# Sparse attention by pairs of heads, values as weights, and the output product in the same stage

## What is computed

```python
q, kc, vc, ks, vs, kw, vw, gates = jnp.split(proj, cuts, axis=-1)
k_cmp = partial_rope(compress(kv_heads(kc), ...), cmp_end)      # 31 compressed keys
p_cmp = masked_softmax(q . k_cmp, cmask);  o_cmp = p_cmp . v_cmp
p_slc = masked_softmax(q . k_sel, smask);  o_slc = p_slc . v_sel
p_win = masked_softmax(q . kw_b, wmask);   o_win = p_win . vw_b
o = gb[..., 0:1] * o_cmp + gb[..., 1:2] * o_slc + gb[..., 2:3] * o_win
return o @ w_out
```

## Time and profile before

| | us |
|---|---|
| median of three runs | 2269.97 |
| lowest and highest | 2268.28, 2273.12 |
| the profiled execution: its time | 2268.3 |
| the profiled execution: its span, first to last instruction | 2266.5 |
| TensorE busy (matmuls) | 2038.2 (90% of the span) |
| VectorE busy | 1384.4 (61%) |
| ScalarE busy | 951.4 (42%) |

### The profile page before, as it was taken

The page is one execution under the profiler, slowest core; times in us unless marked ns, Lnnn a source line. Parts: engine busy times, 40 slices in busy tenths (PEclk is TensorE's granted clock), DMA queues, the critical chain, the costliest instruction groups (busy, mean ns, idle before and its releaser), DMA issues. The chain is left out here.

```text
span 2266.5 us, 29883 instructions
## 1 busy us (share of the span) xinstructions
PE 2038.2 (90%) x11912; PEld 1725.2 (76%) x11912; DVE 1384.4 (61%) x1962; ACT 951.4 (42%) x1399; POOL 147.8 (7%) x206
## 2 busy tenths in 40 slices
PE   5999988969999898999979999699968887799996
PEld 5888878869999786776758888578956666588785
DVE  7964545545454454433468999645036665689997
ACT  5653335221111001623457777421125553477774
POOL 3442000000000000000110001000000000010010
PEclk9999998989999999999979999899879999899998
DMA  7433112214232222221429999432420001199993
GB/s 211 111 73 97 57 57 95 75 29 131 75 111 76 75 76 78 96 93 38 140 68 375 390 394 384 157 89 93 117 77 1 1 1 60 58 354 390 389 381 155
DMA packets 161896, 324.48 MB, mean 143 GB/s; under 512 B 30128, under 2 KB 98416, under 8 KB 161632
## 3 DMA queue, kind: packets, MB, share of 16 engines
q1 hardware_dynamic: 133872, 282.92, 35.7%
q0 software_dynamic: 11488, 31.28, 4.3%
q10 hardware_dynamic: 16400, 8.39, 1.5%
HBM read 299.41 MB, written 17.89 MB: 140 GB/s over the span
## 5 line engine op out<-in xcount | busy, mean ns | idle before, releaser
L2289 PE MATMUL ps<-m_ws,m_xbT 128*128 128x512 f32 x1344 | 314.5, 390 | 0.0
L2289 PEld LDWEIGHTS ps<-m_ws,m_xbT 128*128 128x128 f32 x1344 | 251.8, 188 | 52.2
L2520 DVE TENSOR_TENSOR m_ws<-ring,m_ws 128x2048 fp32r<-128x2048 f32 x112 | 256.1, 2290 | 27.0 <-ACT m_ws L2369 16.3
L1630 PE MATMUL ps<-ffT,ff_ws 128*128 128x264 f32 (+1 forms) x1056 | 241.6, 324 | 4.4 <-DVE ff_ws L433 4.4
L2369 ACT CAST m_ws<-ring 128x2048 fp32r<-128x2048 f32 x112 | 212.9, 1905 | 36.5 <-PE ps L2331 29.7
L1630 PEld LDWEIGHTS ps<-ffT,ff_ws 128*128 128x128 f32 x1056 | 176.8, 190 | 20.2 <-DVE ff_ws L433 4.5
L1630 PE MATMUL ps<-ffT_lo,ff_ws 128*128 128x264 f32 (+1 forms) x528 | 170.3, 322 | 0.0
L2331 PE MATMUL ps<-m_ws,m_hT 128*128 128x512 f32 x672 | 168.8, 401 | 0.0
L2331 PEld LDWEIGHTS ps<-m_ws,m_hT 128*128 128x128 f32 x672 | 123.1, 190 | 23.9
L2517 DVE TENSOR_TENSOR m_ws<-ring,m_ws 128x2048 fp32r<-128x2048 f32 x56 | 128.2, 2289 | 21.4 <-ACT m_ws L2367 21.4
L460 PE MATMUL ps<-fd_ws,fd_xs 128*128 128x512 f32 x528 | 121.8, 393 | 6.7 <-DVE fd_xs L433 6.7
(11 more groups left out here) (540 smaller groups left out, 4288.5 us busy)
## 6 DMA issues: line engine op xcount, KB each, us to landing
ring<-in_moe_w_gate SPq DMA_DIRECT2D x112, 512.0 KB, 5.4
ring<-in_moe_w_up SPq DMA_DIRECT2D x112, 512.0 KB, 7.6
ring<-in_moe_w_down SPq DMA_DIRECT2D x56, 1024.0 KB, 7.7
ring<-in_w_up SPq DMA_DIRECT2D x22, 1024.0 KB, 5.1
ring<-in_w_in SPq DMA_DIRECT2D x16, 1024.0 KB, 6.9
ring<-in_gla_w_in SPq DMA_DIRECT2D x12, 1024.0 KB, 5.3
ring<-in_w_down SPq DMA_DIRECT2D x11, 1024.0 KB, 4.9
ring<-in_nsa_w_in SPq DMA_DIRECT2D x10, 1024.0 KB, 7.7
```

The costliest lines, as they stand in the source:

```text
L1630: ins = nc.tensor.matmul(ps[:, bank, 0:b - a], w[j][:, k, s * P:(s + 1) * P], x[l][:, k, a:b], start=(k == 0 and j == l), stop=(k == KD - ...
L2289: ins = nc.tensor.matmul(ps[:, it % 2, :], xbT[:, blk % 2, a, 4 * half + k, :].bitcast(F32R), v[b][:, k, :], start=(half == 0 and k == 0 a ...
L2520: ins = V.tensor_tensor(o, x.rearrange("p (j k w) -> p j k w", k=4, j=2), x0, ALU.subtract)
```

## The change

The unit of attention becomes a pair of heads and one branch: (u, j, i) with 8 pairs, 2 branches and 4 blocks, again 64 units in the order (0, 3, 1, 2) of the blocks. The two heads of a pair are in the two row halves already, so `qswap` and its DMAs are gone. The reciprocal times the gate is now applied to the probabilities before they are transposed (two operations by VectorE in SBUF, one unit behind the maxima); the transposes follow two iterations behind the scores, the output product three. In the output product the values are the weights (64 columns) and the transposed probabilities stream (128 columns); the result is feature by token, one head in each half of the partitions, and both branches, the compressed branch and all four blocks of a pair add up in one bank of PSUM. The compressed branch keeps only its probabilities, transposed, and its product (512 columns) is the first one into each bank. When a pair is finished ScalarE copies it as the high part and VectorE takes the low part; that is the input of the output product, with no transposes. The output product (`tm_product3`) follows in the same block; its first two slabs of weights are split at iterations 20 and 36 of the loop, the high part by ScalarE. The semaphores are cleared ahead of the attention instead of behind it. The buffers of the probabilities and of their transposes lie in `xT` and in the buffer of the norm's parameters, whose loads by GpSimd wait for the last output product.

```diff
-    def nsa_values_and_compressed(self, m):
+    def nsa_compressed(self, m):
...
-                for it in range(TT + 1):
-                    if it < TT:
-                        pe.wait_ge(p_done, it + 1)
...
-                    i = it - 1
-                    if i >= 0:
-                        pe.wait_ge(t_out, i + 1)
-                        if i >= 2:
-                            pe.wait_ge(o_out, i - 1)
-                        for g in range(NG):
-                            ins = nc.tensor.matmul(ps[:, 4 + 2 * (i % 2) + g // 2, 256 * (g % 2):256 * (g % 2) + 256],
-                                                   pcT[:, i, g, :], vc[:, g, :], start=True, stop=True)
-                        ins.then_inc(o_done, 1)
+                for i in range(TT):
+                    pe.wait_ge(p_done, i + 1)
+                    pe.wait_ge(s_read, TT)
...
-                for g in range(2):
-                    act.dma_start(m["qswap"][64 * g:64 * g + 64], qT[64 - 64 * g:128 - 64 * g]).then_inc(swapped, 16)
...
-                    act.wait_ge(o_done, i + 1)
-                    b = 4 + 2 * (i % 2)
-                    nc.scalar.copy(m["o"][:, i, :].rearrange("p (a c) -> p a c", a=2), ps[:, b:b + 2, :]).then_inc(o_out, 1)
-                act.wait_ge(swapped, 16 * 2)
...
     def nsa_attention(self, m):
...
+            p = m["xT"][:, 0:6].rearrange("p (s e) c -> p s e c", e=2)
+            pT = m["gb"][:].rearrange("p s (e c) -> p s e c", e=2)
+            oh, ol = (sb(ctx, "na_" + n, [P, KD, SEQ]) for n in ("oh", "ol"))
...
+            def transposes_out(eng, n):
+
+                eng.wait_ge(t_out, 2 * n)
+
+            def banks_free(pe):
+                def free(t):
+
+                    if t == 0:
+                        pe.wait_ge(exped, 2 * N)
+                        pe.wait_ge(lo_out, KD - 1)
+                    elif t == 2:
+                        transposes_out(pe, N)
+                    elif t == 3:
+                        pe.wait_ge(lo_out, KD)
+                return free
...
             def _(pe):
-                for it in range(N + 2):
+                for it in range(N + 3):
...
+                        for e in range(2):
+                            r = slice(64 * e, 64 * e + 64)
+                            ins = nc.tensor.matmul(ps[:, 2 * (it % 2) + e, 0:nk], qT[r, u, P * i:P * (i + 1)],
+                                                   kd[r, j, u // 2, 0:nk], start=True, stop=True)
                         ins.then_inc(s_done, 1)
...
+                    n = it - 2
+                    if 0 <= n < N:
+                        i = units[n][2]
+                        if n:
+                            transposes_out(pe, n)
+                        for e in range(2):
+                            pe.wait_ge(scaled, 2 * n + e + 1)
...
+                    n = it - 3
+                    if n >= 0:
+                        u, j, i = units[n]
+                        bank = 6 + u % 2
+                        if n % PAIR == 0:
+                            if u >= 2:
+                                pe.wait_ge(lo_out, u - 1)
+                            nc.tensor.matmul(ps[:, bank, :], vc[:, u // 2, P * (u % 2):P * (u % 2) + P], pcT[:, :, u // 2, :],
+                                             start=True, stop=False)
+                        transposes_out(pe, n + 1)
+                        c = 256 * j + 64 * (u // 2)
+                        for b in range(i + 1):
+                            for e in range(2):
+                                ins = nc.tensor.matmul(ps[64 * e:64 * e + 64, bank, P * i:P * (i + 1)], vsw[:, b, c:c + 64],
+                                                       pT[:, n % 2, e, P * b:P * (b + 1)], start=False, stop=(n % PAIR == PAIR - 1 and b == i))
+                        ins.then_inc(pv_done, 1)
+                self.tm_product3(pe, S, 0, 4, (oh, ol), w_read, y_done, banks_free(pe))
...
             def _(act):
...
+                for it in range(N + 5):
...
+                        if it >= 3:
+                            act.wait_ge(t_done, 2 * (it - 2))
...
+                    n = it - 2
+                    if 0 <= n < N:
+                        nk = P * (units[n][2] + 1)
+                        if n >= 2:
+                            act.wait_ge(pv_done, n - 1)
+                        for e in range(2):
+                            act.wait_ge(t_done, 2 * n + e + 1)
+                            nc.scalar.copy(pT[:, n % 2, e, 0:nk], ps[:, 4 + e, 0:nk]).then_inc(t_out, 1)
+                    n = it - 4
+                    if n >= 0 and n % PAIR == PAIR - 1:
+                        u = n // PAIR
+                        act.wait_ge(pv_done, n + 1)
+                        nc.scalar.copy(oh[:, u].bitcast(F32R), ps[:, 6 + u % 2, :]).then_inc(hi_out, 1)
+                    if it in (20, 36):
+                        S.hi(act, it // 16 - 1)
+                S.hi(act, 2)
+                S.hi(act, 3)
...
             def _(dve):
...
-                        link(V.scalar_tensor_tensor(x, ps[:, 6 + u % 2, 0:64], q[:, 6:7], x, ALU.mult, ALU.add))
-                        V.scalar_tensor_tensor(x, ps[:, 6 + u % 2, 64:128], q[:, 7:8], x, ALU.mult, ALU.add).then_inc(o_out, 1)
...
+                    n = it - 1
+                    if 0 <= n < N:
...
+                        dve.wait_ge(exped, 2 * n + 2)
                         link(V.reciprocal(q[:, 4:6], q[:, 2:4]))
...
+                        for e in range(2):
+                            x = p[:, n % 3, e, 0:nk]
+                            V.tensor_scalar(x, x, q[:, 6 + e:7 + e], None, ALU.mult).then_inc(scaled, 1)
+                    n = it - 5
+                    if n >= 0 and n % PAIR == PAIR - 1:
+                        u = n // PAIR
+                        dve.wait_ge(hi_out, u + 1)
+                        V.tensor_tensor(ol[:, u].bitcast(F32R), ps[:, 6 + u % 2, :], oh[:, u], ALU.subtract).then_inc(lo_out, 1)
+                    if it in (20, 36):
+                        S.lo(dve, it // 16 - 1)
+                S.lo(dve, 2)
+                S.lo(dve, 3)
...
             @block.gpsimd
             def _(pool):
+
+                pool.wait_ge(pv_done, N)
                 for to, frm in m["ln_loads"]:
                     pool.dma_start(to, frm).then_inc(self.ln_in, 16)
```

More of the change, by code:

```diff
@@ new lines, in nsa_attention @@
+            units = [(u, j, i) for u in range(NH // 2) for j in range(2) for i in (0, 3, 1, 2)]
+            N, PAIR = len(units), 8
+            S = Split(W, nc, ws, self.n_no, [2048] * 4, hi_done, lo_done, [(w_read, q + 1) for q in range(4)])
+            self.n_ln += 1
+            block = ctx.enter_context(nc.Block())
+            def transposes_out(eng, n):
[10 more added lines that the diff above has]
+                return free
@@ L3125, in _ @@
             @block.tensor
             def _(pe):
-                for it in range(N + 2):
+                for it in range(N + 3):
                     if it < N:
-                        hd, i = units[it]
+                        u, j, i = units[it]
                         nk = P * (i + 1)
@@ L3132, in _ @@
                             pe.wait_ge(exped, 2 * (it - 1))
-                        for j in range(2):
-                            half = (hd + j) % 2
-                            r = slice(64 * half, 64 * half + 64)
-                            ins = nc.tensor.matmul(ps[:, 2 * (it % 2) + j, 0:nk],
-                                                   (m["qswap"] if j else qT)[r, hd // 2, P * i:P * (i + 1)],
-                                                   kd[r, j, hd // 4, 0:nk], start=True, stop=True)
@@ L3139, in _ @@
-                        ins.then_inc(s_done, 1)
-                    u = it - 1
[L3141 to L3146, removed]
+                        for e in range(2):
+                            r = slice(64 * e, 64 * e + 64)
+                            ins = nc.tensor.matmul(ps[:, 2 * (it % 2) + e, 0:nk], qT[r, u, P * i:P * (i + 1)],
+                                                   kd[r, j, u // 2, 0:nk], start=True, stop=True)
@@ L3149, in _ @@
                                                           self.ident[:])
                             ins.then_inc(t_done, 1)
-                    u = it - 2
-                    if u >= 0:
-                        hd, i = units[u]
-                        if u >= 2:
-                            pe.wait_ge(o_out, u - 1)
-                        for j in range(2):
-                            pe.wait_ge(t_out, 2 * u + j + 1)
-                            c = 256 * j + 64 * (hd // 4)
-                            for b in range(i + 1):
-                                ins = nc.tensor.matmul(ps[:, 6 + u % 2, 64 * j:64 * j + 64], pT[:, u % 2, j, P * b:P * (b + 1)],
-                                                       vsw[:, b, c:c + 64], start=(b == 0), stop=(b == i))
-                        ins.then_inc(o_done, 1)
+                    n = it - 3
@@ L3192, in _ @@
```

(7 more changed lines are left out.)

139 lines of the change are left out of this document (42 added, 97 removed).

## The result

| | before | after |
|---|---|---|
| median, 20 runs each | 2269.4 | 2273.09 |
| lowest and highest | 2264.8, 2273.12 | 2270.51, 2276.93 |
| the profiled execution: its time, its span | 2268.3, 2266.5 | 2271.03, 2269.2 |
| mean granted clock over the span | 0.947 | 0.939 |
| the loop, first product to last output matmul | 198.7 (1693.87 to 1892.53) | 226.5 (1685.51 to 1912.00) |

The ratio is 1.0019, with a 95% interval from 1.0012 to 1.0026: slower by a hair, and within the 0.2% that the prediction called no change. It forecast 2271, between 2257 and 2284. Behind this small difference stand large ones of opposite sign, so the parts are read one by one.

The account below looks back on a forecast made before the run. The prediction took a chain of waits through the engines, with none full, to bound the loop. It summed 26.1 us lost against 24.7 gained, plus 1.4 on 2269.97: 2271 us, range 2257 to 2284.

Parts of the forecast that it names:

- The chain: In the attention loop, links of 6.28 and 6.26 us through all engines: 0.82 more a round, 13.1 us for 16.
- the early start: Behind the loop, the output product starts sooner, minus 12.7 us; rival that this fails: 2277 us, chance 0.04.
- the column halves: In attention's output product two heads stream together, 55 ns a pass; rival without overlap: 109 ns, near 2290, chance 0.08.
- a drain: On TensorE, between full-width and half-width matmuls in the loop: taken as 0.12 us each.
- The splits: Two output-weight slabs split inside the loop, at units 20 and 36: 3 us each, 6 lost in all (0 to 8.4).
- The clock: In the loop, a fifth at 1.2 GHz, each us there costing 0.3: 14 us lost, 7 more than before.
- Outside: Around the loop: minus 10.3 us at the compressed stage, 12.7 at the output product's start, 1.7 for its clock.
- What stood at nothing: Scalings, compressed product, pair copies and differences, POOL's later loads: priced 0, the in-loop pair work at most 1.5 each of eight times.
- Less low clock: Rival: loop waits pull the clock down no more than now, perhaps splits hide: 2264 to 2258 us, chance 0.31.
- The clock staying down: Rival: transposes waiting for both big copies keep the clock low, half the loop: 33 us lost, 2290, chance 0.22.

Follow-up runs that it names:

- e1: Kernel after the change with units in the order 128, 384, 512, 256 keys instead of 128, 512, 256, 384: 2257.8 us, 0.9943 of the kernel before.
- e3: Kernel after the change with the transposes of each head waiting for that head's copy alone, not both: 2267.1 us, 0.9981 of the kernel before.
- e8: Kernel after the change with no slab split inside the loop, all four split behind it: 2275.1 us, 1.0021 of the kernel before.
- e6: Kernel after the change with zero-weight products in TensorE's waits before the transposes of 256 and 128 keys: 2262.7 us, 0.9964 of the kernel before.
- e9: Kernel after the change with order 128, 384, 512, 256, one wait per head, splits at small units, a zero-weight product every second round: 2232.3 us, ratio 0.9825.
- e5: Kernel after the change with both heads' output product in one column half, except each pair's last block: 2288.5 us, 1.0075 of the kernel before.

## Why the prediction was right

The time was forecast at 2271 and came at 2273. The chain, the early start and the column halves were right for the reasons given; the lower clock came near by a price that its working does not give. By its steps:

- **The chain.** Forecast: links of 6.28 and 6.26, a round 0.82 longer, 13.1 for 16. Measured 6.33 and 6.28, 0.89 longer, 14.2. The pass of 55 ns was right; a drain costs 0.14 to 0.16 us (what a group of passes leaves over), not 0.12. (The Trainium skill's page "TensorEngine Tiling (Array Packing)", key properties, says that a change of tiling mode drains TensorE; the trace agrees in that this much is left over between a group in column halves and the next one in row halves, but no run separates the drain from other costs there.) e1 and e3 bear the mechanism out: changing only which copies and outputs meet which exponentials moved the round to 11.4 and 12.3, where 11.5 and 12.3 had been worked out.
- **The splits.** Forecast 3 each, measured 3.84 in the interval: the 1.2 us in which VectorE was to have waited anyway were hardly there. Worth 1.7 in all. e8, without them, has 8.6 us less over 14 rounds, in keeping with the two intervals (7.7).
- **The clock.** Forecast: a fifth of the loop at 1.2 GHz, 7 us more than before; measured 59 us of 226.5, a quarter. Counted over 14 rounds, from the products of 128 keys that open the second round to those that open the sixteenth, the kernel before takes 168.4 us (1707.14 to 1875.55), 4.3 more than 14 rounds of 11.72, and the kernel after 197.4 (1696.33 to 1893.73), 20.9 more than 14 of 12.61. Of these, 7.7 are the splits; the other 13.2 stand against 4.3, so 8.9 more are left for the clock, near the 7 forecast. What lies outside these rounds became 1.2 us shorter. The price was partly luck. The prediction has a round all at 1.2 GHz 3.8 us longer without giving the step: its two rows (1.34 for 0.85) on 4.5 us of chain make 2.6, and even 3.8 on a round that is then 16.3 long is 0.23 for each us spent there, not 0.3. That it costs about a third, 0.33 and 0.36, is shown by e6 and e9.
- **Outside.** 10.3 forecast and 10.3 measured for the compressed stage; 12.7 and 12.85 for the start of the product; 1.7 and 2.2 for its clock (what the product had lost by its slow start was put at 2.1; its own two rows give 2.3). What stood at nothing (scalings, the compressed product, the casts and differences of pairs, POOL's loads behind the last output matmul, at 1912.59 with 43 us of product as cover) shows on no path: the rounds have the length of the links alone.
- **The rivals.** Less low clock was excluded by 59 us. The clock staying down decides, by the prediction's words, from a quarter of the loop on, and a quarter is what came; the measured 0.19% lies on that border. It would take little to have called it slower, so the claim of no change was a close thing. The column halves run together, and e5 is the kernel in which they don't. The early start took place.

What the prediction didn't see is that its largest term wasn't the change's but that of an order of sizes left as it was. The same way of adding up was enough to find it: e1's 11.5 was worked out with it before e1 ran, from durations of the kernel after.

## What to carry to other kernels

When a step of a software pipeline moves to another iteration, work out its chain again for every order of the units: which unit's output meets which unit's long step decides the round, here 12.6 against 11.4 us from the same instructions. Put work for another stage between the units only where the engine's next instruction isn't on that chain, with its two halves in different units, and count what the head start buys behind the loop, clock included. And where a chain leaves TensorE waiting in lumps of 1 to 2 us, price the lower clock from rows at both levels; a product with zeros in the wait can be cheaper than the wait.

## What was unexpected of the hardware

- Two passes with zero weights in a wait, 19 us of additional work on TensorE in e6, made the loop 9.7 us shorter; in e9 one such product in every second round took it from 0.91 to 0.98 of the full clock.
- The waits don't tell the clock by their sum. e5's transposes wait in its loop 47 us for copies and it runs at 0.94, e1's wait 38.5 and it runs at 0.88:

```profile
PE ps L3149 <- ACT ln_gb L3191: 47.2, 30, 3.6
```

```profile
PE ps L3149 <- ACT ln_gb L3190: 38.5, 34, 4.5
```

TensorE is busy for 190 us in e5's loop and for 166 in e1's. What of its work keeps the clock up was not tried further.
